# A second seven-product pair in the first feed-forward layer, its buffers, the attention bias and one copy at the joints

## What is computed

```python
def swiglu(x, w_gate, w_up, w_down):          # 1024 -> 2816 -> 1024, fp32
    return (jax.nn.silu(x @ w_gate) * (x @ w_up)) @ w_down

h = x
f = swiglu(rms_norm(h, ffn1_pre_g), ffn1_w_gate, ffn1_w_up, ffn1_w_down)   # f1
h = h + 0.5 * rms_norm(f, ffn1_post_g)
...                                           # mixer: its softmax adds bias = rpb[...]
```

## Time and profile before

| | us |
|---|---|
| median of three runs (lowest, highest) | 1607.82 (1607.62, 1609.57) |
| the profiled execution, its time | 1610.45 |
| its span from first to last instruction | 1608.6 |
| PE busy in the span | 1586.9 |
| DVE busy, ACT busy, POOL busy | 1122.1, 864.4, 145.9 |
| mean granted PE clock | 0.994 of full speed |

### The profile page before, as it was taken

How to read it: one execution, slowest core, us unless ns; L and a number is a source line. 1 busy time by engine, 2 the same in 40 slices (tenths; PEclk the granted TensorE clock), 3 DMA queues, 4 the chain that set the end, 5 groups by cost and what they waited for, 6 DMA issues and landing times.

```text
span 1608.6 us, 18859 instructions
## 1 busy us (share of the span) xinstructions
PE 1586.9 (99%) x7659; PEld 1322.0 (82%) x7659; DVE 1122.1 (70%) x1081; ACT 864.4 (54%) x907; POOL 145.9 (9%) x148
## 2 busy tenths in 40 slices
PE   9799999999999999999999999999999999999998
PEld 7688888787888888888888888888888998888886
DVE  6784556566995578866468886678856666688864
ACT  6464455745664585653565664356643435555641
POOL 0242000001000001000110100011000032001000
PEclk9899999999999999999999999999999999999999
DMA  9794474359966698953658996698654653689960
GB/s 323 197 265 151 163 269 151 137 198 290 252 183 222 220 258 220 270 209 116 213 189 231 251 249 212 196 290 244 210 218 160 216 182 133 203 260 236 268 209 27
DMA packets 256949, 341.40 MB, mean 212 GB/s; under 512 B 9952, under 2 KB 179168, under 8 KB 256736
## 3 DMA queue, kind: packets, MB, share of 16 engines
q1 hardware_dynamic: 228848, 301.82, 57.1%
q0 software_dynamic: 27648, 38.12, 12.3%
q10 hardware_dynamic: 368, 0.27, 0.1%
HBM read 339.12 MB, written 1.05 MB: 211 GB/s over the span
## 4 chain that ended last, share of the span: by engine, by line
PE 94%; DVE 2%; ACT 2%; DMA 1%; issue 1%; SPq 0%; POOL 0%; DVEq 0%; ACTq 0%
PE bank L846 23%; PE bank L859 23%; PE bank L850 20%; PE bank L908 4%; PE bank L910 4%; PE bank L913 4%; PE bank L796 3%; PE bank L863 3%; PE bank L942 2%; PE bank L945 2%; PE bank L944 2%; ACT split L1449 1%; DVE split L1892 1%; DMA whole<-in_ffn_w_up 1%; DMA whole<-in_gla_w_in 0%
## 5 line engine op out<-in xcount | busy, mean ns | idle before, releaser
L1892 DVE TENSOR_TENSOR split<-whole,split 128x2048 fp32r<-128x2048 f32 (+2 forms) x329 | 705.3, 2162 | 211.4 <-ACT split L1449 210.2
L1449 ACT ACTIVATE split<-whole 128x2048 fp32r<-128x2048 f32 (+1 forms) x313 | 582.6, 1876 | 305.2 <-DMA whole<-in_ffn_w_out 60.9
L846 PE MATMUL bank<-split,xh 128*128 128x512 f32 x1052 | 289.9, 397 | 0.0
L859 PE MATMUL bank<-split,xh 128*128 128x512 f32 x1052 | 283.0, 391 | 3.2 <-DVE split L1892 3.2
L850 PE MATMUL bank<-split,xl 128*128 128x512 f32 x880 | 236.0, 390 | 0.0
L859 PEld LDWEIGHTS bank<-split,xh 128*128 128x128 f32 x1052 | 197.5, 188 | 45.5 <-DVE split L1892 3.9
L846 PEld LDWEIGHTS bank<-split,xh 128*128 128x128 f32 x1052 | 194.4, 189 | 41.0 <-issue 2.8
L850 PEld LDWEIGHTS bank<-split,xl 128*128 128x128 f32 x880 | 165.6, 188 | 35.6
L846 PE MATMUL bank<-split,th 128*128 128x512 f32 x524 | 143.7, 392 | 0.0
L850 PE MATMUL bank<-split,tl 128*128 128x512 f32 x524 | 142.2, 389 | 0.0
L859 PE MATMUL bank<-split,th 128*128 128x512 f32 x524 | 142.1, 389 | 0.0
(11 more groups left out here) (312 smaller groups left out, 1784.0 us busy)
## 6 DMA issues: line engine op xcount, KB each, us to landing
whole<-in_ffn_w_in SPq DMA_DIRECT2D x192, 512.0 KB, 7.5
whole<-in_ffn_w_out SPq DMA_DIRECT2D x40, 1024.0 KB, 5.4
whole<-in_ret_w_in SPq DMA_DIRECT2D x24, 1024.0 KB, 5.1
whole<-in_ffn_w_gate SPq DMA_DIRECT2D x45, 512.0 KB, 6.2
whole<-in_ffn_w_up SPq DMA_DIRECT2D x45, 512.0 KB, 7.7
whole<-in_ffn_w_down SPq DMA_DIRECT2D x20, 1024.0 KB, 5.1
whole<-in_w_in SPq DMA_DIRECT2D x16, 1024.0 KB, 5.4
whole<-in_ffn_w_in POOLq DMA_DIRECT2D x32, 512.0 KB, 8.5
```

What stands on the lines that cost most here:

```text
L846: pe.matmul(o[:, :], tokens(0, k), whi[:, k, :], start=start and k == 0, stop=False, skip_group_check=True)
L859: ins = pe.matmul(o[:, :], tokens(0, k), wlo[:, k, :], start=False, stop=end, skip_group_check=True)
L1449: act.activation(split[s][:, 0:n], whole[r][:, 0:n], ACT.Copy).then_inc(hi.mark(i), 1)
L1892: dve.tensor_tensor(split[r][:, c0:c1], whole[r][:, c0:c1], split[s][:, c0:c1].bitcast(F32), ALU.subtract).then_inc(lo.mark(*what), 1)
```

## The change

`ONE_PAIR` goes, and `f1` takes the list `TWO_PAIRS` as the other layers do: the pairs (3, 4) and (7, 8). Until its down part `f1` may use all 14 blocks. The bias, which lives in two of them, is loaded in `f1`'s down part, after the last use of these two; the loads of gains come behind the accumulating loads on POOL, of which there are now four (`pool_sums`). And the copy of the first tokens moves from `act_lead` to `act_edge`, ahead of the work for t = 1, in the five joints that lead into a feed-forward layer.

```diff
-ONE_PAIR = (
-    ("tile", 0, 0), ("tile", 0, 1), ("tile", 1, 0), ("tile", 1, 1), ("turn", 0),
...
-ONE, TWO = Order(ONE_PAIR, 3), Order(TWO_PAIRS, 3, 7)
-ORDER = {"f1": ONE, "f2": TWO, "a0": TWO, "a1": TWO, "b0": TWO, "b1": TWO}
+TWO = Order(TWO_PAIRS, 3, 7)
+ORDER = {"f1": TWO, "f2": TWO, "a0": TWO, "a1": TWO, "b0": TWO, "b1": TWO}
...
-            give_blocks(lead, end - 8, among)
+            if name == "f1":
+                give_blocks(first, at["f1d"][0], range(14))
+                give_blocks(at["f1d"][0], end - 8, among)
+            else:
+                give_blocks(lead, end - 8, among)
...
         give_ffn("f1", range(12), True)
+        bias_after = max(block_age[12][0], block_age[13][0])
...
-            pool_gain(pool, 1)
-            pool_gain(pool, 2)
...
+            pool_sums(pool, "f1")
+            pool_gain(pool, 1)
+            pool_gain(pool, 2)
             pool.dma_start(mask[:, :], A["c_mask"]).then_inc(bias_in[0].mark("mask"), 16)
+            pool.wait_ge(passed.sem, passed.of(bias_after, 1))
             for n in range(8):
-                if n == 2:
-                    pool_sum(pool, "t1", group["f1", 0].t1)
-                if n == 6:
-                    pool_sum(pool, "t3", group["f1", 0].t3)
-                pool.wait_ge(lo.sem, lo.of(6 + n))
+                pool.wait_ge(lo.sem, lo.of(at["f1d"][n // 2]))
                 pool_bias(0, n)
             for n in range(8):
-                pool.wait_ge(lo.sem, lo.of(14 + n))
+                pool.wait_ge(lo.sem, lo.of(at["f1d"][4 + n // 2]))
                 pool_bias(1, n)
...
             for hd in range(8):
-                pool.wait_ge(lo.sem, lo.of(22 + hd))
+                pool.wait_ge(lo.sem, lo.of(at["f1d"][8 + hd // 2]))
...
             if e.mid:
                 act_high(act, e.mid[-1])
+            if e.nx in ORDER:
+                act_tokens(act, e.nx, 0)
             if units:
                 units(1, 1)
             act_post(act, e, 1)
...
         def act_lead(act, stage, four, unit):
-            if stage in ORDER:
-                act_tokens(act, stage, 0)
```

## The result

| | before | after |
|---|---|---|
| median of the runs (lowest, highest) | 1607.72 (1607.38, 1609.57), 4 | 1596.52 (1596.18, 1597.28), 4 |
| profiled execution, its span | 1610.45, 1608.6 | 1596.24, 1594.1 |
| mean granted PE clock | 0.994 | 0.998 |

The ratio is 0.9929, with a 95% interval of 0.9911 to 0.9946: 11.4 us less (8.7 to 14.3). Forecast were 13.6 less, 1594.2; measured is 1596.5, 2.3 above it, within its range.

A forecast was written before the change was run, and what follows sets the result against it. PE was taken as the bound, busy 1586.9 of 1608.6 us. Matmuls 2.7, first pair 5.8 and joints 5.1 sum to 13.6 us, taken off the median 1607.8 for 1594.2; range 1588.5 to 1601.5.

The forecast's parts named there:

- Matmuls, 2.7: First layer, column blocks 7 and 8: 24 groups become 21, three groups at 0.91 us, 2.7 us less of PE.
- POOL's place: First pair: `t1`'s accumulating load was late because it queued behind the bias on POOL; now issued near 27 us.
- The addend's price: First pair: the accumulating load takes 5.4 us of DMA, moving the seventh tile's landing from 35.9 to 41.3 us.
- The rivals with 35.9 and 44.6: Seventh tile's landing: addend hides, 35.9, time 1588.8 us, chance 0.14; addend starves the queue, 44.6, 1599.2 us, chance 0.13.
- DVE's chain: First pair: 25.8 us on DVE from the seventh tile's landing to split (5, 1), ending 67.1; PE loses 8.2 us.
- The loss before, 14.0: First layer, 46.16 to 69.31 us: PE loses 14.0 us, 9.3 in two waits, the rest half speed.
- The second pair, at nothing: First layer's second pair: 13.8 us more DMA for loads, but 20 us of slack, so no cost.
- the slower rival: First layer, second pair: weights come late, costing 19.9 us, for 1614.1 us; chance 0.05.
- Two more blocks, at nothing: First layer: two more buffer blocks let two loads issue without a wait; nothing beyond the other terms.
- Joints, 5.1: Moving the token copy sooner gains 4.05 us at the joint into `f2`, 1.1 in the turn to `a0`; others nothing.
- The sum off the median: The 13.6 us sum was subtracted from the median 1607.8, giving 1594.2, instead of the profiled 1610.45, giving 1596.9.

The follow-up runs named there:

- e6: Kernel before with one edit: POOL issues the first layer's accumulating loads ahead of gains, mask and bias loads; 1600.03 us, ratio 0.9951.
- e9: The changed kernel run once more without an edit; 1596.87 us, ratio 0.9925 to the kernel before.
- e3: The changed kernel with the copy of the first tokens put back, so the first layer's edits alone; 1601.44 us, ratio 0.9953 to the kernel before.
- e8: The changed kernel with a plain load of the same bytes instead of the accumulating one for `t1`; 1594.20 us, ratio 0.9915 to the kernel before.
- e10: The changed kernel with ACT's gate product of column block 1 ahead of its split of the seventh tile; 1592.81 us, ratio 0.9896 to the kernel before.
- e1: The kernel before, run again without an edit; 1608.80 us, ratio 1.0001.
- e2: The kernel before with only the copy of the first tokens moved sooner; 1605.63 us, ratio 0.9979.
- e4: The changed kernel with first-layer token sums two tiles earlier and ACT's gate product ahead of the seventh tile's split; 1595.16 us, ratio 0.9909 to the kernel before.

## Why the prediction was right, and where it was off

- *Matmuls, 2.7.* The 12 are gone. No run takes them alone.
- *POOL's place.* Right: e6 shows it by that edit only.
- *The addend's price.* Near: the seventh tile at 40.45 for 41.3 (40.92 in e9, 41.84 in e3), by the mechanism named (e8). The rivals with 35.9 and 44.6 are out.
- *DVE's chain.* Right in shape and size: from the seventh tile to the end of the split of (5, 1) 26.1 us for 25.8, ended at 66.5 for 67.1, loss 8.0 for 8.2. What I took as given was its first link, the product with the gate behind ACT's split. I named it and did not price it: it is what e10 takes away, 4.1 us.
- *The loss before, 14.0.* It was that of one execution; e1 and e2 end the first layer 0.6 and 1.0 us sooner with the same instructions, 0.2 to 0.3 of it from their first 46 us.
- *The second pair, at nothing.* Right: PE is busy in every microsecond from 80 to 195, so the slower rival is out.
- *Two more blocks, at nothing.* Half wrong. No run shows a gain by them, but they set ACT's order, which cost about as much as e10 gave back.
- *Joints, 5.1.* The waits went as said, and no joint got a new one. The size was too large: 3.4 by the ratio of e2. 1.6 of it is half speed that only some executions have.
- *The sum off the median.* This is the step that failed in size. The terms were read from an execution 2.6 above the median and belong to it: 1610.45 to 1596.24 are 14.2, for a sum of 13.6. Taken off 1610.45, the sum gave 1596.9, 0.4 from the result. I noted this number and then took the terms off the median, as if none of the 2.6 were in them. That the 13.6 and the 14.2 agree so well is in part luck: in these two executions the joints and `f2` gave 4.5 for 5.1, and the gated attention 1.0 that stood in no term.
- *Not foreseen.* 0.9 us of waiting at L1218, in the gated attention, are gone with the first layer's change (e3, not e2 or e6). The wait was on a small copy that DVE makes behind a split, and that split behind a load. Which shift of the load did it was not tried.

## What to carry to other kernels

A wait and the half speed behind it are in some executions and not in others: a sum from a profiled execution goes against that execution's time, or the part that its clock rows show is taken at less than full. Before buffers or a queue's place are changed, ask which orders the program works out from them; here a changed lead of the splits cost some microseconds, and no run shows that the buffers brought any. And an addend that is issued as early as it can be delays what lands beside it: issued 3.8 us later, so that its bytes moved behind the tile that a chain starts from, it cost that tile nothing (e6).

## What the runs showed of the hardware

- After one and the same wait of 2.19 us, PE's granted clock fell to 0.50 (1.2 GHz) in the profiled executions of before and e3, and stayed at 1.00 (2.4 GHz) in that of e1. It stayed full behind 3.3 us of waiting in e2 and fell behind 3.2 in before. With each of the waits of 4.4 us and more it fell (e1, e2, e3, e4). Four waits of 0.6 to 1.4 us near each other did nothing to it (e10).
- An accumulating load of 1 MiB delayed a load beside it by 4.6, 5.0 and 6.0 us (after, e9, e3), a plain one by 2.7 (e8); while the accumulating one runs, all DMA engines together move 238 to 241 GB/s for 348.
- Two queues with work move about equal numbers of packets: 343 and 379 of about 1 KB each beside the accumulating load, and 217 each beside the plain one, with 0.82 and 0.21 MB (31 to 34 us, after and e8).
- In four executions whose program is the same up to there (after, e3, e9, e10), the sixth tile was split anywhere from 32.19 to 35.62 and the seventh between 40.45 and 41.84: how two queues share shows in the tiles between, less in the last.
